# Two transformer blocks on one core: weight halves take turns with the columns of the products, and row loads move in among the projection's weights

## The chip, the cores and the metric

The kernel runs on one core of one Trainium2 chip. The metric is the device time of one execution in microseconds (us). The engines are named as in the profile: PE is TensorE (PEld its weight loads), DVE is VectorE, ACT is ScalarE, POOL is GpSimd and SP is SyncE. ACT and SP also start transfers (ACTq and SPq rows are those starts).

## What is computed

The input is one sequence of 256 tokens with 1024 features. It passes through a first block of two layers (a state-space group and a gated linear attention, then a feed-forward network, which in the second layer is a mixture of 8 experts), and then a second block of two layers. The change touches the end of the first block and the second block:

```python
def first_block(...):
    for layer in range(DEPTH):
        ...
        f = _moe_swiglu(h, ...)                        # layer 1: the experts
        x = _layer_norm(DN_ALPHA * x + (1 + gt_f) * f, ln_ffn_g[layer], ln_ffn_b[layer])
    return x

def second_block(x, mem, ...):
    for layer in range(DEPTH):
        h = rms_norm(x, mix_norm_g[layer])
        proj = h @ w_in[layer]                         # 1024 x 2720
        ...                                            # three kinds of attention: y_a, y_b, y_c
        y = jnp.concatenate([y_a, y_b, y_c], axis=-1)
        x = x + y @ w_out[layer]                       # 1024 x 1024
        h = rms_norm(x, memx_norm_g[layer])
        x = x + memory_attention(h, mem, ...)
        h = rms_norm(x, ffn_norm_g[layer])
        x = x + jnp.square(jax.nn.relu(h @ w_ff1[layer])) @ w_ff2[layer]
```

## The kernel before

**Weights in two halves.** Every large product is made from three products of rounded numbers. A weight is split into a high half (rounded) and a low half (what the rounding left), and so are the activations. The weights of all layers stand in one planned list (class `Weights`). SP loads them in pieces of 1 MB into a ring of five slots (tile RG). Each piece has two parts of 128x1024. For each part ACT writes the high half (`W.his(a, n)`: WH from RG), DVE subtracts and writes the low half (`W.los(v, n)`: WL from RG and WH), and PE multiplies. There are four such pairs of half buffers for 128x1024 parts, so ACT can prepare four parts ahead, and then each new one waits until PE has used the part four places earlier. SP loads a slot again once DVE has written the low halves of all that lay in it.

**Order.** Each engine runs its own program (`pe_program`, `v_program` for DVE, `a_program` for ACT, `g_program` for POOL, `sp_program`), strictly in the order in which the code issues instructions. A signal from one engine and a wait on another tie them together. `fence(ends)` makes every engine wait until the four compute engines have reached it. Generators (functions with `yield`) are used where two pieces of code are interleaved: `run(strand, n)` issues the next n pieces, `run(strand)` all that are left.

**Where the first block ends.** After the experts a branch is passed (`overflow`; it isn't taken with this data). Then ACT makes the high halves of the first four parts of the next projection, DVE their low halves, and only then DVE starts the layer norm `v_post_ln`. That is a chain between DVE and ACT: DVE multiplies and adds (four column pieces, signalled x00 to x11), ACT sums them ("sum"), DVE makes the mean, ACT sums the squares ("square"), DVE makes the variance ("var"), ACT takes the root ("root"), DVE inverts it and scales X, then DVE and POOL share the gain and bias by columns (`g_post_ln`). A fence follows.

**Where a layer of the second block begins.** After the fence ACT issues the ten transfers of `a_rows2` (rows of gains into tile ROWS, and two small weights that the latent attention uses), and then runs its part of `a_norm`. PE transposes X in four groups of columns into PSUM (`pe_norm`), ACT writes the high half of each group (HTR from PS), DVE the low half (`v_norm`), and PE's projection (`pe_project`) begins when the first two groups have both halves and the first weight part is ready. In `a_project` a high weight half is issued per step, `AHEAD2` of them in each block of 512 columns, followed by the copy of that block's result out of PSUM:

```python
for _ in range(ahead[j]):
    yield
    W.his(a, 1)
yield
a.wait_ge(W.used, parts[-1].i + 1)
```

**Where the attention's output is projected.** After the attention stage's fence PE transposes the joined heads (`pe_heads`, four groups). ACT first makes four high weight halves and then the high halves of the four groups (`a_heads`); DVE first makes four low weight halves and then the four low halves (`v_heads`). PE starts `pe_matmul_out` when all four groups are signalled: in `pe_program` stands

```python
for k0 in range(0, 8, 2):
    pe.wait_ge(cat_v, l, f"l8{k0}")
pe_matmul_out(pe, ("w_out2", l), HT8, 8)
```

Of the kernel before, what the change touches and what calls it, by code (L numbers as in the profile page):

```python
# [18 lines left out]
INC1, INC2 = 2064, 2720  # L19
# [305 lines left out]
def run(strand, pieces=None):  # L325

    if pieces is None:
        for _ in strand:
            pass
    else:  # L330
        for _ in range(pieces):
            next(strand, None)
# [40 lines left out]
def build(nc, w):  # L373
    ctx = ExitStack()
    with ctx:
# [66 lines left out]
        def rowb(ap):  # L442
            return ap.partition_broadcast(128)
# [8 lines left out]
        ACC = AR[:, 6400:8448].rearrange("p (t n) -> p t n", t=2)  # L452
# [289 lines left out]
        def a_project(a, key, cols, PR, ahead, between=lambda j: None, scale=1.0, ready=lambda: None):  # L742
            for j in range((cols + 511) // 512):
                nb = min(512, cols - j * 512)
                parts = W.of[(*key, j)]
# [5 lines that stand above are left out]
                ready()  # L751
                a.act(PR[:, 0, j * 512:j * 512 + nb], PS[:, 4 if j % 2 == 0 else 6, 0:nb], ACT.Copy, scale=scale).then_inc(proj_a)
                between(j)
# [1462 lines left out]
        def rstd(t):  # L2216
            return sm(NST + t, 1)
# [44 lines left out]
        def a_rows2(a, l):  # L2262
            for at, n, name in ((R_LP, 256, "da_lambda"), (R_SUB, 128, "da_subln_g"), (R_SBO, 64, "sb_out_g"),
                                (R_MQ, 96, "mla_q_norm_g"), (R_MK, 96, "mla_k_norm_g"),
                                (R_MO, 64, "mla_out_g"), (R_EQ, 64, "mem_q_norm_g"), (R_EK, 64, "mem_k_norm_g")):
                src = g2(name, l)
                a.dma(ROWS[:, at:at + n], rowb(src.rearrange("a d -> (a d)") if name == "da_lambda" else src)).then_inc(rows_in)
            a.dma(UQ, g2("w_mla_uq", l).rearrange("(k p) n -> p k n", p=128)).then_inc(uw_in)
            a.dma(UKV, g2("w_mla_ukv", l)).then_inc(uw_in)

# [600 lines left out]

        def v_heads(v, r, nb, dst, banks):
            for i, k0 in enumerate(range(0, nb, 2)):
                v.wait_ge(cat_a, r, f"h{nb}{k0}")
                v.tt(dst[1][:, k0:k0 + 2, :], pair(banks[i]), dst[0][:, k0:k0 + 2, :].bitcast(F32), SUB).then_inc(cat_v, f"l{nb}{k0}")

        def a_heads(a, r, nb, dst, banks):
            for i, k0 in enumerate(range(0, nb, 2)):
                a.wait_ge(cat_pe, r, f"p{nb}{k0}")
                a.act(dst[0][:, k0:k0 + 2, :], pair(banks[i]), ACT.Copy).then_inc(cat_a, f"h{nb}{k0}")  # L2880

# [40 lines left out]
        def v_memory(v, l):  # L2922

            W.los(v, 2)
            v.wait_ge(W.used, W.of["mem_q", l][-1].i + 1)
            v.cp(PR2[:, 1, 0:256], PS[:, 1, 0:256]).then_inc(ma_v, "q1")
            v.wait_ge(ma_a, l, "q0")
            q2 = v_rms_sum(v, MQ, 4, view(SCR_ALL[:, :, 0:256], 4), QST)
            for t in range(2):
                v.ts(q2[:, 4 * t:4 * t + 4], q2[:, 4 * t:4 * t + 4], rstd(t), rstd(t), MUL, MUL)  # L2930
            v_root(v, 0, q2, 1.0 / 64, 1e-6, 8).then_inc(ma_v, "rq")
            v.wait_ge(ma_pe, l, "qT")
            v.cp(MQT, pair(2)).then_inc(ma_v, "qT")
            v.wait_ge(ma_a, l, "rq")
            v_rsqrt(v, q2, 0, 8)
            for t in range(2):
                x = v.ts(q2[:, 4 * t:4 * t + 4], q2[:, 4 * t:4 * t + 4], rstd(t), None, MUL)
            x.then_inc(ma_v, "scale")
            for _ in v_attend(v, l, ma_pe, ma_v, ma_a, DST, lambda t: 256, 0, False, (0, 1), (4, 5), 6, AT2, QST):
                pass  # L2940
            v_heads(v, l, 2, oT, (7,))
            W.los(v, 2)
            v_add(v, [W.of["mem_o", l, h][-1] for h in range(2)])

        def a_memory(a, l):
            W.his(a, 2)
            a.wait_ge(W.used, W.of["mem_q", l][-1].i + 1)
            a.act(PR2[:, 0, 0:256], PS[:, 0, 0:256], ACT.Copy).then_inc(ma_a, "q0")
            a_rms(a, ma_v, l, "rq", ma_a, 4, 0)
            a.wait_ge(ma_v, l, "scale")  # L2950
            for _ in a_attend(a, l, ma_pe, ma_v, ma_a, DST, lambda t: 256, (0, 1), (4, 5), ET[:, 0:4], AT2, QST):
                pass
            a_heads(a, l, 2, oT, (7,))
            W.his(a, 2)


# [134 lines left out]
        def v_program(v):  # L3091
            v.ms(COL[:, 0:1], math.pi / 2)
            v.ms(COL[:, 1:2], 1.0)
            v.wait_ge(c_in, 1)
            v.ts(sm(16, 8), CB[:, 0:8], -80.0, None, MAX, None).then_inc(silu_v, "clamped")
            v.wait_ge(silu_a, 1)
            v.ts(sm(16, 8), sm(16, 8), 1.0, None, ADD)
            v.rcp(sm(16, 8), sm(16, 8))
            v.tt(sm(24, 8), CB[:, 0:8], sm(16, 8), MUL)
            v.ms(CZ, 0.0)  # L3100
            v.cp(CZ[:, :, 3], sm(24, 8)).then_inc(silu_v, "c")
            v.wait_ge(consts_in, 1)
            for k in range(8):
                v.ts(CBC[:, k, :], KC[:, K_ONE:K_ONE + 128], sm(24 + k, 1), None, MUL)
            weave(v, "start", p=v_first(v), r=v_s5_first(v))
            for l in range(L):
                if l:
                    run(v_w_in(v, 1))
                v.fence(ends)
                v_mixers(v, l)  # L3110
                v.fence(ends)
                v_out(v, l)
                v.fence(ends)
                if l == 0:
                    v_sums_clear(v)
                    s5w, rest = v_s5_out(v, 1), v_ln_rest(v, 0, X)
                    v_ffn(v, *ffn1()[1:], 7, 0, lambda: run(s5w, 1), lambda n: v_beside(v, n, rest))
                    run(v_post_ln(v, 1, GTF, [W.of["down", 6][-1]] * 2))
                else:
                    v_router(v)  # L3120
                    rest = v_ln_rest(v, 2, H)
                    v_moe(v, W, moe_pe, moe_v, moe_a, 0, lambda e, n: run(rest, 1) if n == 5 else None)
                    overflow(v, "v", lambda: (OW.los(v, 4), v_moe(v, OW, over_pe, over_v, over_a, 1)))
                    W.los(v, 4)
                    run(v_post_ln(v, 3, GTF, None, ACC))
            v.fence(ends)
            for l in range(L):
                v.fence(ends)
                v_norm(v, 3 * l, gcol(0, l))
                run(v_project(v, ("w_in2", l), INC2, PR2, AHEAD2, scale=rstd(1)))  # L3130
                v.fence(ends)
                weave(v, f"attention{l}", b=v_stick(v, l), c=v_latent(v, l), d=v_diff(v, l), k=v_keys(v, l))
                v.fence(ends)
                W.los(v, 4)
                v_heads(v, l, 8, HT8, (4, 5, 6, 7))
                W.los(v, 8)
                v_add(v, [W.of["w_out2", l, h][-1] for h in range(2)])
                v_norm(v, 3 * l + 1, gcol(1, l))
                v_memory(v, l)
                v_norm(v, 3 * l + 2, gcol(2, l), (0, 2, 1, 3))  # L3140
                v_ffn(v, *ffn2(l)[1:], 8, 7 + 8 * l)
                v_add(v, [W.of["ff2", l, 7][-1]] * 2)
            v.done()

        def a_program(a):
# [27 lines left out]
            a.dma(TB, bass.AP(tensor=scratch.tensor, offset=0, ap=[[1, 128], [384, 8], [1, 256]])).then_inc(tb_in)  # L3173
            for l in range(L):
                a.fence(ends)
                a_rows2(a, l)
                a_norm(a, 3 * l, gcol(0, l))
                run(a_project(a, ("w_in2", l), INC2, PR2, AHEAD2, scale=rstd(0), ready=lambda: a.wait_ge(nt_v, 3 * l, "rs")))
                a.fence(ends)
                weave(a, f"attention{l}", b=a_stick(a, l), c=a_latent(a, l), d=a_diff(a, l), k=a_keys(a, l))  # L3180
                a.fence(ends)
                W.his(a, 4)
                a_heads(a, l, 8, HT8, (4, 5, 6, 7))
                W.his(a, 8)
                a_norm(a, 3 * l + 1, gcol(1, l))
                a_memory(a, l)
                a_norm(a, 3 * l + 2, gcol(2, l), (0, 2, 1, 3))
                a_ffn(a, *ffn2(l), 8, 7 + 8 * l, rstd, lambda: a.wait_ge(nt_v, 3 * l + 2, "rs"))
# [93 lines left out]
```

## Time and profile before

| | |
|---|---|
| median of 3 runs | 2976.22 us (2976.21 to 2988.36) |
| the profiled execution | 2977.41 us |
| its span in the profile | 2975.6 us, 31530 instructions |
| PE busy | 2551.3 us (86%) |
| DVE busy | 2060.4 us (69%) |
| ACT busy | 1559.8 us (52%) |
| POOL busy | 23.9 us (1%) |

The profiled execution took 2977.41 us in all, 1.8 us more than its span and 1.2 us more than the median of the runs. Times below are us from the start of that span.

### The profile page before, as it was taken

How to read it: one execution, taken by the hardware profiler on the slowest of the kernel's cores; microseconds unless marked ns; L12 is line 12 of the kernel's file. 1: busy time of each engine (PE TensorE's matmuls, PEld its weight loads, DVE VectorE, ACT ScalarE, POOL GpSimd, SP SyncE). 2: the span in 40 equal slices, each digit the busy share in tenths (PEclk: the TensorE clock that was granted, in tenths of full speed). 3: DMA queues.
4: the chain of work that ended last, by engine and by line, in shares of the span. 5: the costliest groups of instructions: out<-in, count | busy, mean ns of one | idle time of the engine just before them, and what ended most of it. 6: DMA issues, size and time to landing. Idle time of an engine off the chain costs nothing.

```text
span 2975.6 us, 31530 instructions
## 1 busy us (share of the span) xinstructions
PE 2551.3 (86%) x11727; PEld 1998.4 (67%) x11727; DVE 2060.4 (69%) x2214; ACT 1559.8 (52%) x1926; POOL 23.9 (1%) x33
## 2 busy tenths in 40 slices
PE   6987789977968999999999999968686998786898
PEld 2736668855556777777777777756455786555787
DVE  6687786755666888797888888874654554565454
ACT  1222433432146778787777878753534444543443
POOL 0000000000100000000000000000000000000000
PEclk8987999986979999999999999988777999877899
DMA  7450367731336888898989898975012554202352
GB/s 253 159 162 31 113 216 263 270 114 61 101 112 225 325 326 330 293 359 299 344 320 354 329 331 331 335 261 151 15 61 81 164 190 155 95 29 99 100 187 96
DMA packets 274306, 598.03 MB, mean 201 GB/s; under 512 B 28705, under 2 KB 35167, under 8 KB 272993
## 3 DMA queue, kind: packets, MB, share of 16 engines
q1 hardware_dynamic: 252144, 580.30, 55.0%
q10 hardware_dynamic: 22002, 15.66, 2.0%
q8 instruction: 93, 1.52, 0.2%
q14 instruction: 67, 0.55, 0.1%
HBM read 594.86 MB, written 1.06 MB: 200 GB/s over the span
## 4 chain that ended last, share of the span: by engine, by line
PE 61%; DVE 24%; ACT 10%; issue 2%; ACTq 2%; DMA 1%; DVEq 0%; POOL 0%; POOLq 0%; PEldq 0%
PE PS L205 58%; DVE WL L167 8%; ACT WH L197 3%; ACT AR L197 2%; PE PS L213 2%; DVE MW L167 2%; DVE AR L167 2%; ACTq L146 2%; DVE WF L167 1%; DVE MOD L167 1%; ACT MW L197 1%; ACT L197 1%; DVE HF L167 1%; ACT WF L197 1%; DVE SMALL L178 1%
## 5 line engine op out<-in xcount | busy, mean ns | idle before, releaser
L167 DVE TENSOR_TENSOR WL<-RG,WH 128x1024 fp32r<-128x1024 f32 (+1 forms) x558 | 919.4, 1648 | 447.0 <-ACT WH L197 422.2
L197 ACT ACTIVATE WH<-RG 128x1024 fp32r<-128x1024 f32 x782 | 827.4, 1058 | 596.3 <-PE PS L205 527.2
L205 PE MATMUL PS<-WH,HTR 128*128 128x512 f32 (+3 forms) x2920 | 926.1, 393 | 66.8 <-DVE HTR L167 23.4
L205 PEld LDWEIGHTS PS<-WH,HTR 128*128 128x128 f32 x2920 | 557.8, 194 | 201.3 <-DVE WL L167 39.8
L205 PE MATMUL PS<-WL,HTR 128*128 128x512 f32 (+3 forms) x1460 | 569.2, 390 | 0.0
L205 PE MATMUL PS<-WH,ATR 128*128 128x512 f32 x1624 | 522.5, 395 | 16.4 <-DVE WL L167 9.1
L205 PEld LDWEIGHTS PS<-WH,ATR 128*128 128x128 f32 x1624 | 309.4, 191 | 84.4 <-DVE WL L167 18.3
L205 PE MATMUL PS<-MW,HTR 128*128 128x512 f32 x1332 | 331.0, 398 | 18.1 <-DVE MW L167 18.1
L205 PE MATMUL PS<-WL,ATR 128*128 128x512 f32 x812 | 319.6, 394 | 0.0
L205 PEld LDWEIGHTS PS<-WL,HTR 128*128 128x128 f32 x1460 | 282.7, 194 | 52.6
L167 DVE TENSOR_TENSOR MW<-RG,MW 128x2048 fp32r<-128x2048 f32 x112 | 256.7, 2292 | 63.1 <-ACT MW L197 52.5
L205 PEld LDWEIGHTS PS<-MW,HTR 128*128 128x128 f32 x1332 | 249.0, 190 | 70.5 <-DVE MW L167 20.0
L197 ACT ACTIVATE MW<-RG 128x1024 fp32r<-128x1024 f32 x224 | 237.9, 1062 | 24.9 <-PE PS L205 2.2
L213 PE MATMUL PS<-KC,AR 128*128 128x128 f32 (+2 forms) x716 | 118.8, 302 | 69.3 <-DVE AR L167 33.8
L205 PEld LDWEIGHTS PS<-WL,ATR 128*128 128x128 f32 x812 | 154.9, 191 | 31.7
L213 PEld LDWEIGHTS PS<-KC,AR 128*128 128x128 f32 (+2 forms) x716 | 94.9, 157 | 97.4 <-DVE AR L167 40.8
L197 ACT ACTIVATE AR<-PS 128x512 f32<-128x512 f32 (+3 forms) x120 | 66.7, 556 | 118.7 <-PE PS L205 57.9
L197 ACT ACTIVATE AR<-PS,SMALL 128x128 f32<-128x128 f32 (+3 forms) x146 | 77.5, 531 | 73.2 <-PE PS L205 65.0
L197 ACT ACTIVATE ATR<-PS 128x512 fp32r<-128x512 f32 x102 | 61.1, 599 | 81.2 <-PE PS L213 76.2
L205 PE MATMUL PS<-RG,CZ 128*4 128x512 f32 x192 | 93.8, 643 | 10.6 <-DMA RG<-in_mod_w 9.8
L213 PE MATMUL PS<-KC,X 128*128 128x128 f32 x160 | 33.1, 388 | 80.5 <-ACTq L155 30.5
L213 PEld LDWEIGHTS PS<-KC,X 128*128 128x128 f32 x160 | 29.2, 207 | 84.8 <-DVEq L155 36.7
(224 smaller groups left out, 2051.6 us busy)
## 6 DMA issues: line engine op xcount, KB each, us to landing
RG<-in_moe_w_gate SPq DMA_DIRECT2D x112, 1024.0 KB, 5.4
RG<-in_moe_w_up SPq DMA_DIRECT2D x112, 1024.0 KB, 5.6
RG<-in_moe_w_down SPq DMA_DIRECT2D x112, 1024.0 KB, 5.9
RG<-in_w_ff SPq DMA_DIRECT2D x64, 1024.0 KB, 5.2
RG<-in_mod_w SPq DMA_DIRECT2D x48, 1024.0 KB, 5.2
RG<-in_w_in SPq DMA_DIRECT2D x36, 1024.0 KB, 5.2
RG<-in_w_out SPq DMA_DIRECT2D x16, 1024.0 KB, 5.1
RG<-in_ffn_w_gate SPq DMA_DIRECT2D x14, 1024.0 KB, 5.1
```

What stands on the lines that cost most here:

```text
L146: return Ins(self.e.dma_start(dst, src, **kw) if self.e is not None else None, self)
L167: return self.did(lambda: self.e.tensor_tensor(o, a, b, op))
L178: return self.did(lambda: self.e.tensor_reduce(out=o, in_=a, op=op, axis=AX.X))
L197: return self.did(lambda: self.e.activation(o, a, f, bias=bias, scale=scale))
L205: return self.did(lambda: self.e.matmul(o, l, r, start=start, stop=stop))
L213: return self.did(lambda: self.e.transpose(o, a, perm))
```

## The change

Four things are reordered; no computation is added or removed.

1. `a_rows2` becomes a generator that yields after each of its eight row transfers. It is no longer issued before `a_norm`; one piece is issued ahead of each step of `a_project`. The two small weights (`UQ`, `UKV`) go out together in the ninth step.
2. `v_heads` and `a_heads` become generators with a yield ahead of each group, and one weight half is issued ahead of each group instead of four before all.
3. At the end of the first block DVE's four low weight halves move from ahead of the layer norm into it: two after the mean, one after the variance, one after the norm.
4. The two calls in the memory attention run the generators to their end, as before.

```diff
@@ a_rows2
                 a.dma(ROWS[:, at:at + n], rowb(src.rearrange("a d -> (a d)") if name == "da_lambda" else src)).then_inc(rows_in)
+                yield
             a.dma(UQ, g2("w_mla_uq", l).rearrange("(k p) n -> p k n", p=128)).then_inc(uw_in)
             a.dma(UKV, g2("w_mla_ukv", l)).then_inc(uw_in)
@@ v_heads
             for i, k0 in enumerate(range(0, nb, 2)):
+                yield
                 v.wait_ge(cat_a, r, f"h{nb}{k0}")
@@ a_heads
             for i, k0 in enumerate(range(0, nb, 2)):
+                yield
                 a.wait_ge(cat_pe, r, f"p{nb}{k0}")
@@ v_program, end of the first block
-                    W.los(v, 4)
-                    run(v_post_ln(v, 3, GTF, None, ACC))
+                    last = v_post_ln(v, 3, GTF, None, ACC)
+                    run(last, 2)
+                    W.los(v, 2)
+                    run(last, 1)
+                    W.los(v, 1)
+                    run(last)
+                    W.los(v, 1)
@@ v_program, second block
-                W.los(v, 4)
-                v_heads(v, l, 8, HT8, (4, 5, 6, 7))
+                for _ in v_heads(v, l, 8, HT8, (4, 5, 6, 7)):
+                    W.los(v, 1)
@@ a_program, second block
-                a_rows2(a, l)
                 a_norm(a, 3 * l, gcol(0, l))
-                run(a_project(a, ("w_in2", l), INC2, PR2, AHEAD2, scale=rstd(0), ready=lambda: a.wait_ge(nt_v, 3 * l, "rs")))
+                rows2 = a_rows2(a, l)
+                for _ in a_project(a, ("w_in2", l), INC2, PR2, AHEAD2, scale=rstd(0), ready=lambda: a.wait_ge(nt_v, 3 * l, "rs")):
+                    run(rows2, 1)
@@
-                W.his(a, 4)
-                a_heads(a, l, 8, HT8, (4, 5, 6, 7))
+                for _ in a_heads(a, l, 8, HT8, (4, 5, 6, 7)):
+                    W.his(a, 1)
```

DVE's instructions where the first block ends, from the branch to the end of the layer norm (AR holds the experts' sum, MOD the gate, SMALL and ST the statistics):

```order
 L2172 UNCONDITIONAL_BRANCH
-L167 TENSOR_TENSOR WL<-RG,WH 128x1024 x4
 L167 TENSOR_TENSOR AR<-AR,MOD 128x512
...
 L171 TENSOR_SCALAR SMALL<-SMALL 128x2
+L167 TENSOR_TENSOR WL<-RG,WH 128x1024 x2
 L172 TENSOR_SCALAR ST<-SMALL 128x2
+L167 TENSOR_TENSOR WL<-RG,WH 128x1024
 L184 RECIPROCAL SMALL<-ST 128x2
...
 L167 TENSOR_TENSOR X<-X,ROWS 128x704 x2
+L167 TENSOR_TENSOR WL<-RG,WH 128x1024
```

The four low halves (WL) stood ahead of the norm's first multiplication. Now they stand behind the mean, behind the variance and behind the last column piece.

ACT's instructions where the first layer of the second block begins (HTR is the normalised input, of which PE waits for the halves; the second layer reads the same):

```order
 L146 DMA MOD<-bias_scratch 128x8x256
-L146 DMA ROWS<-in_da_lambda 128x256
-L146 DMA ROWS<-in_da_subln_g 128x128
...
-L146 DMA ROWS<-in_w_mla_ukv 128x512
 L197 ACTIVATE HTR<-PS,SMALL 128x256 x8
 L198 ACTIVATE AR,SMALL<-X 128x1024 x2
 L197 ACTIVATE ST<-ST 128x2
-L197 ACTIVATE WH<-RG 128x1024 x4
+L146 DMA ROWS<-in_da_lambda 128x256
+L197 ACTIVATE WH<-RG 128x1024
+L146 DMA ROWS<-in_da_subln_g 128x128
+L197 ACTIVATE WH<-RG 128x1024
```

Ten transfer starts stood ahead of the norm's eight activations. Now the norm comes first, and a start stands ahead of each of the next high halves.

DVE's instructions where the output projection begins (HTR is here the joined heads):

```order
 L181 COPY MOD<-PS 128x512
-L167 TENSOR_TENSOR WL<-RG,WH 128x1024 x4
-L167 TENSOR_TENSOR HTR<-PS,HTR 128x512 x4
+L167 TENSOR_TENSOR WL<-RG,WH 128x1024
+L167 TENSOR_TENSOR HTR<-PS,HTR 128x512
...
+L167 TENSOR_TENSOR WL<-RG,WH 128x1024
+L167 TENSOR_TENSOR HTR<-PS,HTR 128x512
 L167 TENSOR_TENSOR WL<-RG,WH 128x1024 x8
 L167 TENSOR_TENSOR X<-X,PS 128x512 x4
```

Four and four have become pairs of one and one; the last one of the eight is a group of the heads in either order.

## Rows read from the trace of the kernel before

**Rows 1.** The page: the span, and the chain that ended last, by engine

```profile
span 2975.6 us, 31530 instructions
PE 61%; DVE 24%; ACT 10%; issue 2%; ACTq 2%; DMA 1%; DVEq 0%; POOL 0%; POOLq 0%; PEldq 0%
```

**Rows 2.** Timeline, end of the first block: start, us, engine, instructions [idle before <-releaser]

```profile
1987.20 4.38 ACT L197 ACTIVATE WH<-RG 128x1024 fp32r<-128x1024 f32 x4 [3.73 <-issue]
1991.83 5.21 DVE L167 TENSOR_TENSOR WL<-RG,WH 128x1024 fp32r<-128x1024 f32 x4 [4.05 <-ACT WH L197]
...
2004.04 1.15 ACT L198 ACTIVATE H<-X,SMALL 128x1024 f32<-128x1024 f32 x1 [0.43 <-DVE SMALL L171]
...
2006.58 0.17 DVE L172 TENSOR_SCALAR ST<-SMALL 128x2 f32<-128x2 f32 x1 [2.58 <-ACT H L198]
2006.63 1.28 ACT L197 ACT_TABLE_LOAD   x1
...
2008.16 0.17 DVE L184 RECIPROCAL SMALL<-ST 128x2 f32<-128x2 f32 x1 [1.40 <-ACT ST L197]
...
2013.52 2.36 DVE L167 TENSOR_TENSOR X<-X,ROWS 128x704 f32<-128x704 f32 x2
2013.57 3.03 POOL L167 TENSOR_TENSOR X<-X,ROWS 128x320 f32<-128x320 f32 x2 [0.63 <-DVE X L172]
```

**Rows 3.** The branch's line: duration ns min/median/max, start us

```profile
L2172 DVEq COMPARE_BRANCH  x1: 72/72/72, 1988.8 to 1988.8; - x1
```

**Rows 4.** Tile ROWS: duration ns min/median/max, first and last start, forms

```profile
L167 DVE TENSOR_TENSOR X<-X,ROWS x12: 892/1224/1430, 397.3 to 2014.4; 128x1024 f32<-128x1024 f32 x8, 128x704 f32<-128x704 f32 x4
L205 PE MATMUL PS<-ROWS,HF x24: 486/591/1219, 2096.6 to 2581.8; 128*128 128x384 f32 x16, 128*128 128x512 f32 x8
```

**Rows 5.** Timeline, first layer of the second block

```profile
2017.34 3.31 PE L213 MATMUL PS<-KC,X 128*128 128x128 f32 x16 [30.48 <-ACTq L155]
2017.38 0.44 ACTq L146 DMA_DIRECT2D ROWS<-in_da_lambda  x1
...
2022.62 4.20 ACT L197 ACTIVATE HTR<-PS,SMALL 128x256 fp32r<-128x256 f32 x8 [14.50 <-issue]
...
2025.91 0.79 PE L205 MATMUL PS<-WH,HTR 128*128 128x512 f32 x1 [5.26 <-DVE HTR L175]
```

**Rows 6.** Timeline, second layer of the second block

```profile
2496.01 3.68 PE L213 MATMUL PS<-KC,X 128*128 128x128 f32 x16 [5.42 <-POOLq L155]
...
2500.88 4.20 ACT L197 ACTIVATE HTR<-PS,SMALL 128x256 fp32r<-128x256 f32 x8 [9.19 <-issue]
...
2504.16 0.80 PE L205 MATMUL PS<-WH,HTR 128*128 128x512 f32 x1 [4.48 <-DVE HTR L175]
```

**Rows 7.** Waits, 2026 to 2085: who waited for whom, us in total, times, longest

```profile
ACT WH L197 <- PE PS L205: 26.7, 18, 1.7
```

**Rows 8.** Windows: us, busy PE PEld DVE ACT POOL, PE clock granted, DMA share, GB/s

```profile
2017.30:2020.70 3.40, 3.31 (x16) 3.10 (x16) 0.00 (x0) 0.00 (x0) 0.00 (x0) 0.58 0.83 208
...
2025.90:2030.35 4.45, 4.44 (x11) 3.47 (x12) 2.70 (x9) 3.39 (x7) 0.00 (x0) 0.50 0.84 179
2030.35:2082.00 51.65, 51.65 (x229) 42.80 (x228) 24.33 (x23) 21.21 (x22) 0.00 (x0) 1.00 0.51 170
...
2504.16:2508.30 4.14, 4.14 (x10) 3.31 (x11) 2.43 (x7) 3.38 (x7) 0.00 (x0) 0.50 0.34 129
...
2084.00:2203.00 119.00, 86.64 (x354) 57.94 (x353) 81.53 (x172) 56.67 (x123) 0.00 (x0) 0.78 0.08 27
```

**Rows 9.** Timeline, output projection of the first layer

```profile
2204.53 5.21 DVE L167 TENSOR_TENSOR WL<-RG,WH 128x1024 fp32r<-128x1024 f32 x4 [1.33 <-ACT WH L197]
2207.82 2.66 ACT L197 ACTIVATE HTR<-PS 128x512 fp32r<-128x512 f32 x4
2209.85 3.08 DVE L167 TENSOR_TENSOR HTR<-PS,HTR 128x512 fp32r<-128x512 f32 x4
```

**Rows 10.** DMA issues, 2016 to 2060: KB each, median us to landing

```profile
ROWS<-in_w_mla_ukv ACTq DMA_DIRECT2D x1, 256.0 KB, 8.8
```

More of the change, by code:

```diff
@@ L2940, in v_memory @@
                 pass
-            v_heads(v, l, 2, oT, (7,))
+            run(v_heads(v, l, 2, oT, (7,)))
             W.los(v, 2)
@@ L2952, in a_memory @@
                 pass
-            a_heads(a, l, 2, oT, (7,))
+            run(a_heads(a, l, 2, oT, (7,)))
             W.his(a, 2)
```

## The prediction

> **What bounds the kernel now.** I read the page first. The chain that ended last is PE for 61% of its length, DVE for 24% and ACT for 10% [rows 1], so most of the time is products, and a change that adds or removes none can only work where PE stands still. The diff names three such places, so I read the timeline of each, and for each asked one thing: which engine's last instruction does PE, or the fence ahead of PE, wait for?
>
> *The end of the first block.* PE stands still from the experts' end to 2017.34, for 30.48 us [rows 5]. The reader is to see a single thread that goes from DVE to ACT and back, and at its head the four low halves: they run from 1991.83 for 5.21 us, and the norm's first multiplication comes behind them [rows 2]. DVE is on the path all that time, and no product needs those halves before 2025.91 [rows 5].
>
> *The beginning of a layer of the second block.* PE's 16 transposes start at 2017.34, but ACT copies their result only at 2022.62, since it starts ten transfers from 2017.38 on [rows 5]. The second layer has the same picture: transposes from 2496.01, ACT's first copy at 2500.88, first product at 2504.16 [rows 6].
>
> *The output projection.* DVE makes four low halves (5.21 us) and then the four groups of the heads (3.08 us), back to back, while ACT has long finished its groups [rows 9].
>
> **Edit 1, the low halves at the end of the first block.** From when could DVE start the norm, if the halves didn't stand there? The row says that WL waited 4.05 us for ACT's WH. But WL needs only the first high half, which was there at 1987.20 + 4.38/4 = 1988.3 [rows 2], and DVE's branch ended at 1988.9 [rows 3]. ACT shows an idle time of 3.73 us with no releaser at the same branch [rows 2]. I choose: what lies between 1988.9 and 1991.83 is what an engine takes to go on after that branch, and any first instruction starts at 1991.83. The norm then starts 5.2 us earlier. (If the row were right, and DVE could go on at 1988.9, it would be 8.1 us; this is the upper bound.)
>
> Where do the halves go? One takes 5.21/4 = 1.30 us. Two stand beside ACT's sums of squares, which take from 2004.04 to 2006.58, 2.54 us [rows 2]: 2.6 us, a delay of 0.1. One stands between the variance's end (2006.58 + 0.17 = 2006.75) and the inversion at 2008.16, 1.41 us in which ACT loads a table and takes the root [rows 2]: 1.30 fits, no delay. The last stands behind DVE's last column piece, which ends at 2013.52 + 2.36 = 2015.88, while POOL ends at 2013.57 + 3.03 = 2016.60 [rows 2]. The fence behind it waited for POOL. Now it waits for DVE: 2015.88 + 1.30 = 2017.2, 0.6 us later. For its first 0.7 us this half runs beside POOL. DVE's pieces of 704 columns show what that costs: 0.89 us at the least, 1.43 at the most, within one pair beside POOL [rows 4]. At that rate 0.7 us costs another 0.3. I take 0.75, with 0.6 and 0.9 as its bounds.
> By the Trainium skill (SBUF — State Buffer, "Who interferes with whom") VectorE and GpSimd share one pair of ports, which the one that started first holds for its whole instruction, and an operation with two SBUF inputs is of the kind that blocks. By that rule the last half would wait for POOL's end and finish at 2017.9, 1.3 us late; this rule speaks against the place of that half, and the row shows a slowing rather than a stop.
> Sum of this edit: -5.2 + 0.1 + 0.75 = **-4.4 us** (-3.9 to -7.3).
>
> SP reloads a slot only when its low halves are written, so four reloads come up to some 14 us later. The parts they bring are used some ten parts later, at 2.7 us each behind 2025.91, so I cost this at nothing; with that cover gone a reload costs its landing.
>
> **Edit 2, the row loads.** ACT can copy when the first four of 16 transposes are done: 3.31/4 = 0.83 us behind 2017.34, with a handover of 0.1 that is 2018.25 instead of 2022.62 [rows 5]: -4.4 us. In the second layer 3.68/4 = 0.92 behind 2496.01 gives 2497.0 instead of 2500.88 [rows 6]: -3.9 us. From then on ACT's own pace decides (4.20/4 = 1.05 us a group, slower than the transposes), and the first product follows ACT's first copy by 3.29 us and 3.28 us, as now [rows 5, 6].
>
> The ten starts don't vanish; what hides them? In the projection ACT waits for PE before nearly each high half, 18 times and 26.7 us, 1.5 us each [rows 7]. A start of 0.44 us [rows 5], or the two together in the ninth step, fit in there, ahead of a wait which ends with PE and not with ACT. PE is busy for 51.65 of 51.65 us behind its slow beginning [rows 8], so the stage shifts as a whole. The data are late by some 25 us: the last small weight is started near 2045 and lands within 9 us [rows 10], and PE first uses them at 2096.6 [rows 4]. Without this cover it would be a wait at the head of the latent attention.
>
> **The clock on top.** PE's granted clock is 0.50 of full, 1.2 GHz, in the first 4.45 us of products of the first layer and in the first 4.14 of the second [rows 8]. Ahead of these PE transposed for 3.31 us and then stood still for 5.26. Late in the transposes the grant had risen (mean 0.58), and it was gone again when the products came [rows 5, 8]. Now the gap between transposes and first product shrinks to 0.83 + 0.1 + 3.29 - 3.31 = 0.9 us. At full clock from the start, half of 4.45 and of 4.14 would go, 2.2 + 2.1 = 4.3 us; if nothing changes, 0. Since the grant did rise in the first layer's transposes, I take 2.0 there, and only 1.0 in the second: **-3.0 us**.
> The Trainium skill (TensorE: Matmul & The Clock Gate, "What's actually happening") says that the throttled state is the default and that activity releases it. By that, a denser beginning can only help, and the sum would be nearer to its end of 4.3; the trace agrees in the first layer's transposes.
>
> **Edit 3, the output projection.** Nothing. PE waits for all four groups. DVE's work ahead of the last is the same eight instructions, 5.21 + 3.08 us, in either order, and DVE doesn't wait in between, for ACT's pair takes 4.38/4 + 2.66/4 = 1.76 us and DVE's 2.07 [rows 2, 9]. The pairing would pay if PE could start with the first group, and its wait isn't changed. The calls in the memory attention issue what they did.
>
> **Sum.** -4.4 (first block's end) - 4.4 - 3.9 (the starts) - 3.0 (clock) = -15.7 us. The profiled execution took 2977.41 us, so 2961.7; the median of the runs is 1.2 below that execution, so **2960.5 us**. Half a per cent, which is about what a measurement of this kernel tells from no change, is 14.9 us: the forecast stands right beside it.
>
> **The rivals.**
> *The clock gives nothing, or as much is lost later.* All that follows is shifted, and the attention stages run on a mean grant of 0.78 with PE busy for 87 of 119 us [rows 8], so where the clock rises in them can move. For: the second layer's transposes came before products that ran at 0.50. Against: the gap that stood between is nearly gone. The time: 2976.2 - 12.7 = 2963.5.
> *The last half's place, or the branch, eats edit 1.* If another engine is what releases the fence, or DVE's first instruction isn't ready at 1991.83, only the starts and some clock stay: -8.3 - 3.0 gives 2964.9. Against: nothing else is busy there.
> *More than forecast.* DVE goes on right behind the branch (2.9 us more), and the clock gives its full 4.3: 2960.5 - 4.2 = 2956.3. For: the releaser that the row names.
> *Slower: the attention loses the clock.* A shift could keep PE at half clock for longer in the two attention stages. One hundredth of mean grant over such a stage is about 0.87/0.78 = 1.1 us of the PE work on its path, at most. The 12.7 us are gone from when the mean falls by 6 hundredths in both, from 0.78 to 0.72; below 0.65 the kernel is over 0.5% slower, near 2992. Against: stages alike in both layers show grants of their own that hang on their gaps, and those the change doesn't touch.
> *Nothing changes*, if ACT or DVE wait there for something that the trace doesn't name: 2976.2. Against: the ten starts stand one behind the other with no wait among them.
>
> **How the numbers follow.** Forecast with part of the clock 0.50; clock nothing 0.28; edit 1 eaten 0.08; more than forecast 0.09; slower 0.02; nothing 0.03. The range for 8 in 10 takes in the first two with the bounds of their terms, and most of the third and fourth: 2954.5 to 2967. Faster by over 0.5% means below 2961.3: most of the forecast's case and of "more", a small part of "clock nothing", together 0.53. Slower by over 0.5%: 0.02. Within: 0.45.
>
> **What would show it.** In the changed kernel's timeline DVE's AR<-AR,MOD should start about 3 us behind the branch's end at 1988.9; two WL beside ACT's squares; X done at 2015.9 - 5.1 and the transposes 4.4 us earlier, near 2012.9. ACT's HTR copies should follow the transposes' start by 0.9 us and the first product by 4.2, in both layers, with ROWS starts between the high halves and ACT still released by PE. The output projections should take from DVE's first WL to the first product what they do now, 8.7 us. I'd be wrong if WL or the fence lay on the path elsewhere, if a high half waited for a landing, or if the windows of the attention stages show another clock than 0.78.

## The result

The changed kernel takes 2971.01 us (median of 19 runs, 2956.24 to 2977.07), the kernel before 2981.75 us (19 runs, 2970.77 to 2988.36). The ratio is 0.9962, with a 95% interval of 0.9953 to 0.9971: some 11 us, 0.4%, faster. Forecast were 2960.5 us in a range of 2954.5 to 2967, and a gain of 15.7 us. The time lies above the range. One execution of one kernel below (edit 1 alone), 3247.73 us at a mean granted clock of 0.756, is left out of all numbers.

The page of the changed kernel reads like the one before [rows 1]:

```profile
span 2969.2 us, 31523 instructions
PE 60%; DVE 25%; ACT 10%; issue 2%; ACTq 1%; DMA 1%; DVEq 0%; POOLq 0%; PEldq 0%
```

ACTq has gone from 2% to 1% of the chain. The places themselves say more. The end of the first block, in the changed kernel's timeline [before: rows 2]:

```profile
1989.95 3.31 DVE L175 SCALAR_TENSOR_TENSOR AR<-PS,SMALL,AR 128x512 f32<-128x512 f32 x4
1997.18 0.69 DVE L167 TENSOR_TENSOR AR<-AR,MOD 128x512 f32<-128x512 f32 x1 [3.91 <-issue]
...
2004.22 2.55 DVE L167 TENSOR_TENSOR WL<-RG,WH 128x1024 fp32r<-128x1024 f32 x2
...
2007.15 1.23 DVE L167 TENSOR_TENSOR WL<-RG,WH 128x1024 fp32r<-128x1024 f32 x1
2008.48 0.17 DVE L184 RECIPROCAL SMALL<-ST 128x2 f32<-128x2 f32 x1
...
2013.88 3.03 POOL L167 TENSOR_TENSOR X<-X,ROWS 128x320 f32<-128x320 f32 x2 [0.63 <-DVE X L172]
...
2016.30 1.69 DVE L167 TENSOR_TENSOR WL<-RG,WH 128x1024 fp32r<-128x1024 f32 x1
```

The reader is to see three things. The norm's first multiplication now comes 3.92 us behind the end of the experts' last sum (1993.26), and nothing is named as its releaser: that is what going on behind the branch takes (2.81 us of it lie behind the end of DVE's branch row). Three halves lie beside ACT's work and cost 0.2 us together (from the norm's first multiplication to DVE's last column pieces, X<-X,ROWS, it takes 16.66 us instead of 16.44). The fourth runs beside POOL and takes 1.69 us instead of 1.23. It ends at 2017.99, 1.1 us behind POOL's 2016.91.

The beginnings of the two layers, in the changed kernel [before: rows 5, 6]:

```profile
2018.66 3.63 PE L213 MATMUL PS<-KC,X 128*128 128x128 f32 x16 [26.32 <-ACTq L155]
...
2019.87 4.21 ACT L197 ACTIVATE HTR<-PS,SMALL 128x256 fp32r<-128x256 f32 x8 [11.64 <-PE PS L213]
...
2023.16 0.50 PE L205 MATMUL PS<-WH,HTR 128*128 128x512 f32 x1 [0.86 <-DVE HTR L175]
...
2491.01 3.68 PE L213 MATMUL PS<-KC,X 128*128 128x128 f32 x16 [5.42 <-POOLq L155]
...
2495.54 0.80 PE L205 MATMUL PS<-WH,HTR 128*128 128x512 f32 x1 [0.85 <-DVE HTR L175]
```

ACT is now released by PE's transposes, and PE waits 0.9 us for the first halves instead of 5.3 and 4.5. A first product of 0.50 us in the first layer and of 0.80 in the second tells the clock: full in one, half in the other. The ten starts lie in ACT's waits for PE. Two rows of the changed kernel's timeline show one of them:

```profile
2028.43 0.33 ACTq L146 DMA_DIRECT2D ROWS<-in_da_subln_g  x1
2028.93 1.06 ACT L197 ACTIVATE WH<-RG 128x1024 fp32r<-128x1024 f32 x1 [0.53 <-PE PS L205]
```

And the changed kernel's waits from 2023 to 2082 [before: rows 7]:

```profile
ACT WH L197 <- PE PS L205: 23.9, 17, 1.7
```

For the comparison of single executions I cut them at events: T is the first transpose of a layer, P its first product, H the end of DVE's last copy ahead of the output projection, Q that projection's first product, X DVE's first addition behind it. All in us, worked out from timelines like the ones above; "last sum" is the end of DVE's last sum of the experts. The program ahead of it is the same in all kernels.

| stretch | before | changed | gain | forecast |
|---|---|---|---|---|
| last sum to T, first layer | 29.56 | 25.40 | 4.16 | 4.4 |
| T to P, first layer | 8.57 | 4.50 | 4.07 | 4.4 |
| P to H, first layer | 177.29 | 174.70 | 2.59 | 2.0 (clock) |
| H to Q, first layer | 9.99 | 9.98 | 0.01 | 0 |
| Q to T of the second layer | 282.82 | 283.17 | -0.35 | 0 |
| T to P, second layer | 8.15 | 4.53 | 3.62 | 3.9 |
| P to H, second layer | 176.45 | 177.09 | -0.64 | 1.0 (clock) |
| H to Q, second layer | 9.99 | 9.98 | 0.01 | 0 |
| Q to the end | 285.00 | 286.59 | -1.59 | 0 |
| last sum to the end | 987.82 | 975.94 | 11.88 | 15.7 |

The last line agrees with the ratio (0.0038 x 2982 = 11.3 us). The 1.6 us that are lost behind the last output projection lie mostly at one place. Windows of the kernel before and then of the changed one, both from 70 us behind X of the second layer, over the beginning of the last feed-forward:

```profile
2787.60:2797.60 10.00, 6.79 (x29) 5.49 (x28) 5.50 (x7) 3.83 (x7) 0.00 (x0) 0.83 0.64 211
2797.60:2837.60 40.00, 40.00 (x183) 33.18 (x182) 21.41 (x21) 19.70 (x21) 0.00 (x0) 1.00 0.50 159
```

```profile
2779.51:2789.51 10.00, 6.80 (x24) 5.38 (x23) 5.27 (x7) 3.62 (x5) 0.00 (x0) 0.69 0.63 211
2789.51:2829.51 40.00, 40.00 (x181) 33.13 (x180) 21.32 (x20) 18.82 (x20) 0.00 (x0) 0.99 0.49 158
```

PE is busy for the same 6.8 and 40 us in both, but does less in them: its grant is 0.83 and 1.00 before, 0.69 and 0.99 after. (0.83 - 0.69) x 10 + 0.01 x 40 = 1.8 us of full clock, about what is missing.

### The profile page after: what moved, and what is told of

Read it like the earlier page. It is cut to its first block, busy times and chain, and to the rows that moved or that the text cites. A ratio compares the mean times of both kernels' runs of the same rounds, so it can differ in the third digit from the quotient of the medians.

```text
span 2969.2 us, 31523 instructions
## 1 busy us (share of the span) xinstructions
PE 2551.0 (86%) x11727; PEld 1994.7 (67%) x11727; DVE 2060.6 (69%) x2214; ACT 1560.2 (53%) x1926; POOL 24.0 (1%) x33
## 4 chain that ended last, share of the span: by engine, by line
PE 60%; DVE 25%; ACT 10%; issue 2%; ACTq 1%; DMA 1%; DVEq 0%; POOLq 0%; PEldq 0%
PE PS L205 57%; DVE WL L167 8%; ACT WH L197 3%; PE PS L213 2%; ACT AR L197 2%; DVE MW L167 2%; DVE AR L167 2%; DVE WF L167 1%; ACTq L146 1%; DVE MOD L167 1%; ACT MW L197 1%; DVE HF L167 1%; ACT L197 1%; DVE HTR L167 1%; DVE SMALL L178 1%
## 5 line engine op out<-in xcount | busy, mean ns | idle before, releaser
L205 PE MATMUL PS<-RG,CZ 128*4 128x512 f32 x192 | 95.9, 655 | 10.5 <-DMA RG<-in_mod_w 9.8
```

The source lines that it names most:

```text
L205: return self.did(lambda: self.e.matmul(o, l, r, start=start, stop=stop))
```

## The experiments

| kernel | ratio to before | 95% interval | last sum to T | T to P (1st, 2nd layer) | H to Q (both) | last sum to end |
|---|---|---|---|---|---|---|
| before, once more | 0.9995 | 0.9986 to 1.0005 | 29.40 | 8.24, 8.17 | 9.99, 9.98 | 987.81 |
| changed | 0.9962 | 0.9953 to 0.9971 | 25.40 | 4.50, 4.53 | 9.98, 9.98 | 975.94 |
| edit 2 alone (row loads) | 0.9974 | 0.9964 to 0.9985 | 29.40 | 4.50, 4.52 | 9.98, 10.01 | 976.06 |
| edit 1 alone (low halves) | 0.9991 | 0.9981 to 1.0 | 25.37 | 11.02, 8.08 | 9.98, 9.98 | 986.85 |
| edit 3 alone (pairing) | 1.0003 | 0.9994 to 1.0012 | 29.59 | 8.28, 8.14 | 9.98, 9.99 | 987.89 |
| edit 1 as two and two | 1.0003 | 0.9992 to 1.0013 | 25.69 | 8.24, 8.19 | 9.99, 9.98 | 985.09 |
| changed, half behind the fence | 0.9956 | 0.9942 to 0.9971 | 24.37 | 4.39, 4.53 | 9.98, 9.99 | 971.65 |
| changed, PE kept warm | 0.9952 | 0.9939 to 0.9966 | 26.46 | 4.50, 4.07 | 9.99, 9.98 | 975.49 |
| changed, PE waits by group | 0.9893 | 0.9876 to 0.9911 | 25.40 | 4.49, 4.52 | 3.45, 3.44 | 959.88 |
| by group, unpaired | 0.9926 | 0.9913 to 0.994 | 25.38 | 4.49, 4.52 | 7.39, 7.40 | 966.77 |
| by group, half behind the fence | 0.9898 | 0.9884 to 0.9913 | 24.51 | 4.39, 4.53 | 3.44, 3.45 | 961.11 |
| the same, PE kept warm | 0.9882 | 0.9867 to 0.9897 | 24.38 | 3.93, 4.07 | 3.44, 3.45 | 956.52 |

**Before, once more.** The kernel before, unchanged.

> The kernel before, unchanged, as if it were a change. It tells what the comparison can tell from nothing: a ratio of 1.000 within 0.001, single runs that lie up to 15 us apart and follow the mean granted clock. Its stages behind the experts should repeat to 0.1 us those of the kernel before: 29.6, 8.6, 10.0 and 10.0. Rival (the stages vary by themselves as much as the edits move them): they differ by 1 us or more.

The ratio is 0.9995 (0.9986 to 1.0005), and from the last sum to the end the profiled executions took 987.82 and 987.81 us. What differed by 3.5 us was when the last sum ended (1987.78 and 1991.29). Single stretches repeat less well than the 0.1 us that were expected: the last sum to T took 29.40 us instead of 29.56, T to P of the first layer 8.24 instead of 8.57, and P to H 177.69 instead of 177.29, and these happen to cancel. So for one and the same kernel a profiled execution measures the stages behind the experts more sharply than its whole time does. Between kernels this doesn't hold where the granted clock comes in: see "The clock of the first products" below.

**The edits one by one.** Each is the kernel before with that part of the change's diff and no other.

> The kernel before with edit 2 alone (row loads among the projection's weights). Measured from the start of PE's transposes to the first product: 4.5 us in both layers instead of 8.6 and 8.2, as in the changed kernel (theory: the ten starts were on the path and now are hidden behind ACT's wait for PE), which is 7.7 us together. On top, the granted clock of the first products is full in one layer or the other, worth 0 to 2 us each. Whole kernel 0.25 to 0.4% faster. Rival (the starts are only moved, and stand in the projection's path): the projection up to the attention becomes 4 us longer and the time stays.

The stretches came as expected, 8.6 to 4.50 and 8.2 to 4.52. The whole is 0.26% faster (0.9974), and the first theory holds. From the last sum to the end this kernel took 976.06 us, as little as the changed kernel with 975.94, although T of the first layer comes 4.0 us later in it. That is luck with the clock: its profiled execution is the fastest of its ten (2965.41 us, median 2974.30), its first products ran at full clock in both layers, and P to H of the second layer took 173.26 us instead of 177.09.

> The kernel before with edit 1 alone (low halves inside the layer norm). From the end of the experts' last sum to PE's transposes: 25.4 us instead of 29.6, in which the norm's first multiplication comes 3.9 us behind the sum's end; everything behind it as before, so 4.2 us, 0.14%. Rival (the branch was not what held DVE): the multiplication comes right behind the branch, about 1 us behind the sum's end, and the gain is 7 us.

The norm starts 3.88 us behind the last sum, and 4.2 us are won up to T, as in the first theory; the rival, a gain of 7 us, falls. But they are not kept: T to P takes 11.02 us, 2.5 us longer than before. Both theories had missed it. By the ratio (0.9991) edit 1 alone is worth 2.7 us, with an interval from nothing to 5.7. SP's and ACT's starts in this kernel's timeline (x2 and 21.75 us: the second of SP's two starts comes at 2040.75):

```profile
2019.37 21.75 SPq L146 DMA_DIRECT2D RG<-in_w_in  x2
```

```profile
2019.47 0.40 ACTq L146 DMA_DIRECT2D MOD<-bias_scratch  x1
...
2021.67 1.21 ACTq L146 DMA_DIRECT2D ROWS<-in_mla_q_norm_g  x1
...
2025.47 2.23 ACTq L146 DMA_DIRECT2D ROWS<-in_w_mla_ukv  x1
2027.75 4.20 ACT L197 ACTIVATE HTR<-PS,SMALL 128x256 fp32r<-128x256 f32 x8 [18.17 <-issue]
```

The last low half frees a weight slot. It is now written just ahead of the fence, so SP starts that slot's 1 MB at 2019.37, and ACT its own 1 MB (the bias table) at 2019.47. Behind these two, single starts of ACT take up to 2.23 us, and the ten of them 7.7 us instead of 5.2. To test this, the halves were put two and two, so that the slot is free 8.3 us sooner (SP's start then comes 16.4 us behind the last sum, and 24.7 with edit 1):

```diff
                     last = v_post_ln(v, 3, GTF, None, ACC)
                     run(last, 2)
                     W.los(v, 2)
                     run(last, 1)
-                    W.los(v, 1)
+                    W.los(v, 2)
                     run(last)
-                    W.los(v, 1)
```

> The kernel before (starts ahead of the norm) with the low halves inside the layer norm two and two, behind the mean and behind the variance, so that the last reload of a weight slot starts some 9 us earlier than with edit 1. Theory (with edit 1 alone that reload, started 0.1 us ahead of a 1 MB transfer on ACT, made the ten starts take 7.7 us instead of 5.2): the ten starts take 5.2 us again, transposes to first product 8.6 us instead of 11.0; from the experts' last sum to the transposes 25.8 instead of 25.4. Rival (the starts were slow by chance in that execution): also near 11 us, or it varies without the reload.

The last start is quick again, in that kernel's timeline:

```profile
2022.94 0.44 ACTq L146 DMA_DIRECT2D ROWS<-in_da_lambda  x1
...
2027.31 0.49 ACTq L146 DMA_DIRECT2D ROWS<-in_w_mla_ukv  x1
2027.85 4.20 ACT L197 ACTIVATE HTR<-PS,SMALL 128x256 fp32r<-128x256 f32 x8 [15.71 <-issue]
```

4.9 us for the ten, and T to P is 8.24. So where the reload falls decides it; one profiled execution of each says so, and the whole times (0.9991 and 1.0003) are too coarse to confirm it. The other kernels fit: the ten starts take 5.2, 4.9 and 4.9 us in the kernel before, in its repetition and with edit 3 alone, where no reload falls there. The bias table lands 8.5 us behind its start with edit 1 alone and 8.4 in the changed kernel, where the reload starts 0.1 us ahead of it too, and after 5.3 to 5.6 us in the three kernels just named and with the halves two and two. In the changed kernel the same collision costs nothing up to P, since the starts no longer stand ahead of the norm.

> The kernel before with edit 3 alone (one weight half ahead of each group of the heads). Theory: from the heads' copy to PE's first product 10.0 us as before in both layers, and no difference in the whole. Rival (the pairing lets PE begin sooner, or makes DVE wait for ACT): that stretch becomes shorter by 1 us or more, or longer.

No stretch differs from the kernel before by more than 0.3 us, and the ratio is 1.0003: edit 3 is worth nothing, as the first theory had it.

**Making the pairing pay.** The changed kernel, with PE's wait moved:

```diff
-                for k0 in range(0, 8, 2):
-                    pe.wait_ge(cat_v, l, f"l8{k0}")
-                pe_matmul_out(pe, ("w_out2", l), HT8, 8)
+                pe_matmul_out(pe, ("w_out2", l), HT8, 8, lambda k: pe.wait_ge(cat_v, l, f"l8{k // 2 * 2}"))
@@ pe_matmul_out(pe, key, src, kt, ready)
                 for p in W.of[(*key, h)]:
+                    for k in range(p.kk):
+                        ready(p.k0 + k)
                     pe.wait_ge(W.lo, p.los)
```

> The changed kernel, in which PE also waits for one group of the heads ahead of the weight part that uses it, instead of for all four ahead of the first. Theory: the pairing then pays. DVE's first pair is ready 2.1 us into its 8.5, so the first product comes about 6.4 us sooner in each layer (3.6 us from the heads' copy instead of 10.0), and since a part takes PE 2.7 us or more and DVE's next pair 2.1, PE doesn't stop again: 9 to 13 us for both layers, 0.3 to 0.4% against the changed kernel, 0.7 to 0.8% against the one before. Rival (the output projection is bound by the weights' halves, not by its start): the first product comes sooner, but PE waits in between and DVE's addition of X comes at the same time.

The first product of the first layer comes 3.45 us behind the copy instead of 9.98. DVE and PE in this kernel's timeline:

```profile
2197.41 1.23 DVE L167 TENSOR_TENSOR WL<-RG,WH 128x1024 fp32r<-128x1024 f32 x1 [1.33 <-ACT WH L197]
2198.74 0.69 DVE L167 TENSOR_TENSOR HTR<-PS,HTR 128x512 fp32r<-128x512 f32 x1
2199.54 1.23 DVE L167 TENSOR_TENSOR WL<-RG,WH 128x1024 fp32r<-128x1024 f32 x1
...
2199.53 0.78 PE L205 MATMUL PS<-WH,HTR 128*128 128x512 f32 x1
```

PE starts behind DVE's first pair. From its first product to DVE's addition it now takes 24.93 us instead of 27.06, so the rival, that it would only wait in between, falls. The reason is the clock. The first 5 us of products in the changed kernel and in this one (windows):

```profile
2207.84:2212.80 4.96, 4.96 (x12) 3.90 (x13) 0.00 (x0) 0.00 (x0) 0.00 (x0) 0.50 0.35 105
```

```profile
2199.53:2204.50 4.97, 4.97 (x22) 4.10 (x21) 4.54 (x5) 4.55 (x6) 0.00 (x0) 0.91 0.35 107
```

They run on a grant of 0.50 behind a pause of 6.2 us, and on 0.91 without the pause: (0.91 - 0.50) x 5 us = 2.1 us. The Trainium skill (TensorE: Matmul & The Clock Gate, "What's actually happening") says that activity releases the throttle; the trace agrees here. Altogether the stretch from the last sum to the end is 16.1 us shorter than in the changed kernel, where 9 to 13 were expected, and the kernel 1.07% faster than before instead of 0.7 to 0.8%: the two starts gave 13.1 us, and the clock of the products behind them, which the expectation didn't count, another 3.8 us up to DVE's additions, of which 0.9 was lost elsewhere.

> Edits 1 and 2, the old order at the output projection (four weight halves, then four groups), and PE waiting group by group. It tells what the pairing is worth once PE waits so. Theory: the first group's low half is then DVE's fifth instruction, ready 5.21 + 0.08 + 0.69 = 6.0 us into its 8.5, so from the heads' copy to the first product 7.6 us instead of 10.0 (none of the change's pairing) and 3.4 (pairing and group wait): 2.4 us a layer of the 6.5. Rival (the wait alone made the gain): 3.4 us here too.

This is the kernel above without edit 3. H to Q takes 7.39 us (7.6 were expected): the wait by groups is worth 2.6 us a layer by itself, the pairing another 3.9. The pause ahead of the first product is 3.6 us here, the grant of the first 5 us of products 0.60, and first product to DVE's addition takes 26.38 us, between the other two.

**The last half behind the fence.**

```diff
-                    W.los(v, 1)
             v.fence(ends)
             for l in range(L):
                 v.fence(ends)
+                if l == 0:
+                    W.los(v, 1)
                 v_norm(v, 3 * l, gcol(0, l))
```

> The changed kernel, with the last of the four low halves behind the fence instead of ahead of it. Theory: that half held the fence (it ran 1.69 us beside POOL instead of 1.23 and ended 1.1 us behind POOL), and behind the fence DVE waits for ACT's first HTR group anyway. From the norm's first multiplication to PE's transposes 20.5 us instead of 21.5, transposes to first product 4.5 as before: 1.0 us, too little for the whole time to tell. Rival (the fence is held by something else, or the half delays the first HTR low half): no change, or the loss comes back between the transposes and the first product.

From the norm's first multiplication to T it takes 20.48 us instead of 21.48, and T to P stays (4.39): 1.0 us, as expected. That the stretch to the end was 4.3 us shorter in this execution has another cause: 4.0 us of it lie between P and H of the second layer (173.04 us against 177.09), which edit 2 alone shows too (173.26).

**The clock of the first products.** This is the first product of the second layer in this kernel's timeline; in the changed kernel the same row reads 0.80:

```profile
2490.05 0.50 PE L205 MATMUL PS<-WH,HTR 128*128 128x512 f32 x1 [0.85 <-DVE HTR L175]
```

The eight kernels with edit 2 run the same program from T to H of the second layer (two of them with PE kept warm ahead of it, see below). With edit 2 alone, with the half behind the fence and with the unpaired wait the grant is 1.00 in the first 4.3 us behind P, and P to H takes 173.26, 173.04 and 173.04 us. In the changed kernel, with the group wait, and with both improvements it is 0.50, and P to H takes 177.09, 177.10 and 177.12. Product by product, 2.0 us of the 4.0 arise in the first ten products and most of the rest at later places, near 112 and near 143 us behind P, where PE again runs at half clock in one kernel and at full clock in the other. In the first layer it is alike, with less at stake: 174.70 to 175.50 us at a grant of 1.00 (five kernels), 176.48 to 176.68 at 0.50 to 0.59 (three). In all of them PE waits 0.7 to 0.9 us between the transposes and P, unless it is kept warm. What decides between the two levels is not shown. A single profiled execution can thus lie 4 us off in one stretch without any cause in the edit.

Both of these diffs on the changed kernel:

> The changed kernel with both improvements: PE waits group by group in the output projection, and the last low half is behind the fence. Theory: the two add up, 16 us (measured for the first from the experts' end on) and 1.0 us: from the experts' last sum to the end 959 us. Whole kernel 1.1% faster than before. Rival (they share a cover): only one of the two.

The places add up (24.51 and 3.44), but the sum to the end is 961.11 us instead of the 959 expected and isn't below the 959.88 of the kernel with the group wait alone. P to H of the first layer takes 176.48 us instead of 174.97, on a grant of 0.53 instead of 1.00 in its first 4.3 us. A gain of 1 us drowns in what the clock does elsewhere.

**PE kept warm.**

```diff
+                    pe.wait_ge(ln_v, 3, "n0")
+                    for i in range(28):
+                        pe.tr(PS[:, 4, 0:128], KC[:, K_ONE:K_ONE + 128], IDN)
             pe.fence(ends)
             for l in range(L):
+                if l:
+                    for i in range(22):
+                        pe.tr(PS[:, 4, 0:128], KC[:, K_ONE:K_ONE + 128], IDN)
                 pe.fence(ends)
```

> The changed kernel, with transposes of constants on PE in its idle time ahead of the fence, 28 in the first layer of the second block and 22 in the second; nothing reads their result. Theory (the clock term): the grant is then full when the products begin in both layers. In the second layer, where the changed kernel began at 0.50, the projection's first products get 2 us shorter; in the first layer, where it was full already, nothing. From the transposes of the second layer to the heads' copy 179.5 us instead of 181.6. Rival (what limits the first products is something else than the clock): granted clock 1.0 there and no shorter.

The transposes of the second layer did run at full clock, but the products not wholly. PE stood still for 2.1 us between them, ran the first products at full clock and was at half clock 2 us behind P. Windows of the two:

```profile
2493.10:2496.70 3.60, 1.96 (x16) 1.73 (x16) 1.52 (x4) 2.54 (x6) 0.00 (x0) 1.00 0.38 148
2497.17:2501.40 4.23, 4.23 (x13) 3.35 (x14) 2.52 (x8) 3.38 (x7) 0.00 (x0) 0.67 0.01 2
```

From T to H of the second layer it took 178.2 us, and 179.5 were expected against 181.6. But edit 2 alone has 177.8 there without any such help.

In the first layer the expectation failed. Nothing was to change there, but the grant of the first products was 0.50, where the changed kernel has 1.00:

```profile
2010.23 5.07 PE L213 MATMUL PS<-KC 128*128 128x128 f32 x28 [18.71 <-DVE X L172]
2018.77 3.65 PE L213 MATMUL PS<-KC,X 128*128 128x128 f32 x16 [3.47 <-ACTq L155]
2023.27 0.79 PE L205 MATMUL PS<-WH,HTR 128*128 128x512 f32 x1 [0.85 <-DVE HTR L175]
```

The 28 extra transposes ended 3.5 us ahead of the real ones, and P to H took 176.68 us instead of 174.70. So more work of PE ahead of the fence did not bring the full clock by itself, and 975.49 us from the last sum to the end are no gain. (1.1 us of the last sum to T, 26.46 against 25.40, lie behind the branch, where DVE took 3.86 us instead of 2.81.)

And all three diffs on the changed kernel:

> The changed kernel with PE waiting group by group, the last low half behind the fence, and the transposes of constants ahead of the fences. Theory: from the experts' last sum to the end 961.1 us (without those transposes) minus 2 to 3.5 for the second layer's first products: 958. The time 1.1 to 1.2% under the one before. Rival (PE's extra work delays the fence or shifts the clock elsewhere): 961 or more.

It took 956.52 us, 1.5 less than expected, of which 0.9 us may be T to P (3.93 and 4.07 us instead of 4.39 and 4.53), as ACT's first copy comes 0.8 us behind T instead of 1.2 when the first transposes run at full clock; the time is 2949.64 us, a ratio of 0.9882 (0.9867 to 0.9897). It is the fastest of all, but its interval overlaps with that of the kernel with the group wait alone (0.9876 to 0.9911).

## Why the prediction was wrong

Two steps failed: the base from which the gain was taken, by 5.5 us, and within the gain the clock term, by 3.0. What the three edits do by themselves was forecast rightly, to 0.9 us of 12.7.

**The base.** The largest single step that failed is the one from the gain to the time: "the median of the runs is 1.2 below that execution, so 2960.5 us". It stood on three runs of which two agreed within 0.01 us (2976.21 and 2976.22), and I took that for the kernel's precision, though the third stood 12 us above them. With 19 runs the same kernel has a median of 2981.75, 5.5 us higher, and single runs from 2970.77 to 2988.36. Of the 10.5 us between forecast and result this is half. The other half is the gain, 15.7 forecast and 10.7 between the two medians.

**The clock term.** "Since the grant did rise in the first layer's transposes, I take 2.0 there, and only 1.0 in the second: -3.0 us." The traces show nothing of the 3.0 in the sum: 2.6 us won in the first layer, 0.6 lost in the second, and another 2 us lost further on, of which 1.6 in the last feed-forward. The step that had no support is that a shorter gap between transposes and products brings the full clock. The gap did shrink to 0.9 us in both layers, as forecast, and the first products ran on 1.00 in one and on 0.50 in the other; other kernels with about the same gap show either level in either layer. The rival "the clock gives nothing, or as much is lost later", with a chance of 0.28 and a gain of 12.7, describes what happened. That the profiled execution shows nothing, and not some 4 us, is luck; over all runs the ratio, 11.3 us, leaves nothing for the clock either. The stages of attention as such kept their clock: from 56 us behind P to H the grant is 0.78 and 0.77 in the changed kernel as before, so the rival in which they lose it did not come true.

**The terms of the edits: -12.7 forecast, -11.9 in the traces.** With the clock at nothing this is the whole gain in the traces (11.88 us; 11.3 by the ratio).
- Edit 1, "any first instruction starts at 1991.83", holds: 3.92 us behind the last sum, with "issue" for a releaser. It gave 4.16 instead of 4.4: the norm starts 5.4 us sooner instead of 5.2, the three hidden halves cost 0.2 instead of 0.1, and the last one held the fence for 1.1 us instead of 0.75. By the row the half should have been slowed by 0.3 us beside POOL; it was slowed by 0.46, of the 0.61 us that POOL still worked. By the rule of the Trainium skill (SBUF — State Buffer, "Who interferes with whom") it would have waited for POOL's end at 2016.91 and ended at 2018.14; it ended at 2017.99, between the rule's end and the row's (2017.83), as far from one as from the other. The upper bound of 8.1 and its rival fell. The bound of 3.9 below doesn't follow from its terms, which give -5.2 + 0.1 + 0.9 = -4.2.
- Edit 2 gave 4.07 and 3.62 instead of 4.4 and 3.9. ACT's first copy comes 1.21 and 1.23 us behind the first transpose, where I had 0.93 and 1.02, a quarter of the 16 and 0.1 us for the handover.
- Edit 3 gave nothing, for the reason given, and the group wait showed that PE's wait was the reason.

**The interplay.** That edit 1 moves a weight reload onto ACT's starts was in the prediction only as "four reloads come up to some 14 us later ... I cost this at nothing". There are two, since a piece of 1 MB has two parts, and counted from the last sum they come 6.9 and 15.5 us later. The second collides with ACT's transfers. That it cost nothing up to P was so only because edit 2 takes the starts away. Alone, edit 1 lost 2.5 of its 4.2 us there.

## What to carry to other kernels

An order of instructions pays only as far as the waits around it allow. Pairing halves with the columns that products wait for gave nothing until PE's wait was split in the same way, and then 3.9 us of the 6.5 per layer that the two gave together. When a piece of work is moved, also ask when the buffers that it frees come free, and what starts then. A clock that depends on what PE did before is no term to count on: it moved one stretch by 4 us between kernels that run the same program there, so compare stretches with the granted clock beside them, and don't credit an edit with what the clock gave. And before a gain is turned into a time, look at how far single runs of the same program lie apart; with three runs the base was off by half the gain.

## What the runs showed of the hardware

Single executions of one and the same program on one core differ. The 19 of the changed kernel run from 2956.24 us at a mean granted clock of 0.914 to 2977.07 at 0.906, and over the 19 the correlation of time and mean grant, worked out from their results, is -0.84. In the profiled executions the difference arises mostly ahead of the experts: their first weights are started at 829.9 us in the kernel before, and at 827.0 and 837.1 in two other kernels that are the same up to there.

PE's clock can stand at either level, 1.2 or 2.4 GHz (a grant of 0.50 or 1.00), behind the same 16 transposes and the same wait of 0.9 us, and P to H of the second layer then takes 177.1 or 173.0 to 173.3 us.

Behind a branch that isn't taken DVE needs 2.78 to 2.97 us from the end of the branch's row to its first instruction in twelve of the thirteen profiles, and 3.86 in the other, and ACT 2.4 to 2.8, with nothing named as a releaser.

A single transfer start on ACT took 2.23 us, against 0.49 for the same instruction in other executions, behind two transfers of 1 MB that SP and ACT had started within 0.1 us.
